# Two layers of a hybrid decoder on one core: the prompt's queries and keys are transposed in the projection, into the place of x, and the prompt's compression moves into retention

## The reference

```python
u = rmsnorm(x, norm_pre) @ w_in            # 3872 columns: ret q,k,v,g | nsa q,kv,gates | gdn qkv,...
# retention: 4 heads, a state carried over the tiles of the prompt, per sample for the samples
# gated DeltaNet: 4 heads, behind a convolution of width 4
# NSA, prompt: 8 query heads in 2 groups (4 heads share one key/value head), head size 64
k_c = compress(rows[:, :, 0]); v_c = compress(rows[:, :, 1])   # 31 blocks of 32 positions
o = gate0 * attend(q, k_c, v_c) + gate1 * attend(rope(q), k_sel, v_sel) + gate2 * attend(rope(q), k_win, v_win)
x = x + rmsnorm(concat(ret, nsa, gdn) @ w_out, norm_post)
```

## Time and profile before

| | |
|---|---|
| time, median of 3 runs | 2633.17 us (2610.85 to 2634.86) |
| profiled execution | 2642.13 us, its span 2640.5 us |
| mean granted TensorE clock of that execution | 0.854 |
| busy: PE / PEld / DVE / ACT / POOL | 84% / 63% / 50% / 28% / 11% |
| read from HBM, written | 223.17 MB, 24.97 MB |

### The profile page before, as it was taken

One profiled execution on the slowest core, in us unless ns is written; L12 is line 12 of the kernel. 1 busy time (PEld: TensorE's weight loads), 2 busy tenths in 40 slices (PEclk: granted clock), 3 DMA queues, 4 the chain that ended last, 5 costly groups with the idle time before them and its releaser, 6 DMA issues. The chain is left out here.

```text
span 2640.5 us, 35927 instructions
## 1 busy us (share of the span) xinstructions
PE 2229.7 (84%) x12280; PEld 1657.8 (63%) x12280; DVE 1321.1 (50%) x3088; ACT 730.7 (28%) x1512; POOL 302.4 (11%) x516
## 2 busy tenths in 40 slices
PE   6989748738999999997889896586499999999977
PEld 3644448737767888886354444486376678888863
DVE  1252566534654666654213434765355556666532
ACT  2120002103434454440212101111044445444302
POOL 0000000000013433420000000000000234334100
PEclk9999769756879999996989997687567889999859
DMA  4443010020027886851035330100300368868420
GB/s 148 147 151 113 26 35 1 1 79 7 1 52 168 192 188 152 181 124 72 2 113 168 137 109 10 35 1 2 84 1 1 89 150 191 179 152 190 107 72 36
DMA packets 175947, 242.04 MB, mean 92 GB/s; under 512 B 50118, under 2 KB 132838, under 8 KB 175084
## 3 DMA queue, kind: packets, MB, share of 16 engines
q1 hardware_dynamic: 151180, 172.51, 24.5%
q0 software_dynamic: 24576, 67.14, 10.8%
HBM read 223.17 MB, written 24.97 MB: 94 GB/s over the span
## 5 line engine op out<-in xcount | busy, mean ns | idle before, releaser
L601 PE MATMUL bank<-W,hT 128*128 128x512 f32 (+3 forms) x1152 | 449.0, 544 | 30.6 <-DMA W<-in_w_in 21.5
L1282 POOL DMA_DIRECT2D SHARED<-in_cache_nsa_kv x256 | 151.5, 592 | 2048.7 <-issue 734.4
L601 PEld LDWEIGHTS bank<-W,hT 128*128 128x128 f32 x1152 | 219.0, 195 | 230.8 <-issue 184.5
L1225 PE MATMUL bank<-XT,W 128*128 128x256 f32 (+1 forms) x768 | 250.8, 462 | 0.0
L1214 ACT ACTIVATE XT<-bank 128x512 f32<-128x512 f32 x256 | 140.3, 593 | 132.6 <-PE bank L1207 132.5
L1282 POOL DMA_DIRECT2D PS<-in_cache_nsa_kv x256 | 150.7, 589 | 140.6 <-issue 128.2
L1225 PEld LDWEIGHTS bank<-XT,W 128*128 128x128 f32 x768 | 134.9, 190 | 49.7 <-issue 36.9
L1207 PE MATMUL bank<-CF,RP 128*128 128x128 f32 x1024 | 146.9, 290 | 7.6 <-DVE RP L1195 6.9
L1708 PE MATMUL bank<-QBD,PS 128*128 128x64 f32 x1024 | 141.9, 287 | 0.0
L1501 DVE TENSOR_REDUCE mx<-bank 128x1 f32<-128x31 f32 (+4 forms) x192 | 74.6, 389 | 132.5 <-PE bank L1443 131.1
L1708 PEld LDWEIGHTS bank<-QBD,PS 128*128 128x128 f32 x1024 | 139.7, 210 | 0.7
(11 more groups left out here) (378 smaller groups left out, 3699.4 us busy)
## 6 DMA issues: line engine op xcount, KB each, us to landing
SHARED<-in_cache_nsa_kv SPq DMA_DIRECT2D x256, 128.0 KB, 6.1
SHARED<-in_cache_nsa_kv POOLq DMA_DIRECT2D x256, 128.0 KB, 5.3
PS<-in_cache_nsa_kv SPq DMA_DIRECT2D x256, 128.0 KB, 6.1
PS<-in_cache_nsa_kv POOLq DMA_DIRECT2D x256, 128.0 KB, 5.7
W<-in_w_in SPq DMA_DIRECT2D x48, 512.0 KB, 4.5
XS<-scratch_conv_p SPq DMA_DIRECT2D x24, 384.0 KB
PW<-in_state_nsa_win SPq DMA_DIRECT2D x16, 512.0 KB, 3.8
Wo<-in_w_out SPq DMA_DIRECT2D x4, 2048.0 KB, 11.8
```

The costliest lines, as they stand in the source:

```text
L601: return nc.tensor.matmul(bk((c * NTILE + t) % 8)[:, 0:b - a], hT[:, k, t * P:(t + 1) * P], W[:, k // 2, k % 2, 0:b - a], start=(k == 0), ...
L1225: mm = nc_(self.v).tensor.matmul(out, self.v['W1'][:, kv, s, :], seg[:, s], start=(s == 0), stop=(s == SEG // PAIRS - 1))
L1282: e.dma_start(where[side * HD:(side + 1) * HD, slot, :, :], A['cache_nsa_kv'][l, page].rearrange("(p r) a g d -> p r (a g d)", r=PAIRS)[:, ...
```

## The change

x leaves the core after its transposition: `X` is stored to `q_rot` and, for the sample rows, to `y_sample`, and `out_project` loads it back behind `w_out`. Its place holds `QT` [128, 2, 4, 512] and `KT` [128, 2, 512] until then. In `project`, the rotated queries of tiles 0 to 2 go to MIX, those of tile 3 to `QR`; bank 7 is taken from the ring (8 banks become 7) and 8 key transposes (beside chunk 7) and 32 query transposes (beside chunk 8) go through it, copied out by ScalarE. In `retention`, the prompt's compression and the loading of its weights run beside the tiles, at the places of the table `BESIDE`. The early stage of `prompt_attention` is gone. In its main stage both groups share one `KT` and one `KC`: group 0 in rows 0 to 63, group 1 in rows 64 to 127, so a score product has the 64 rows of its group. The branches run in the order 1, 2, 0.

```diff
@@ project
-    NC, RING = len(chunks), 4
+    NC, RING, BANKS, TURNS = len(chunks), 4, 7, 7
+    q_rows = lambda t: MIX[:, t, :].rearrange("p (i c) -> p i c", i=2) if t < 3 else QR[:, :, :]
@@ SP
+            e.dma_start(A['q_rot'].rearrange("(t p) d -> p t d", p=P), X[:, 0:4, :]).then_inc(kept, 16)
+            e.dma_start(O['y_sample'].rearrange("b t d -> (b t) d"), X[0:64, 4, :]).then_inc(kept, 16)
...
-                dve.wait(e, f"nqc{j}")
-                e.dma_start(A['q_rot'][j * P:(j + 1) * P, :], QR[:, :, :].rearrange("p i c -> p (i c)")).then_inc(rot, 16)
@@ ACT
+            copies(e, 6, 0)
+            e.wait_ge(kept, 32)
+            for t in range(4):
+                pe.wait(e, f"tk{t}")
+                act.done(e, f"tk{t}", nc.scalar.activation(KT[:, :, t * P:(t + 1) * P], bk(TURNS, 4)[:, 0:2, :], ACT.Copy))
+            copies(e, 7, 0)
+            for t in range(4):
+                for i in range(2):
+                    pe.wait(e, f"tq{t}{i}")
+                    act.done(e, f"tq{t}{i}", nc.scalar.activation(QT[:, i, :, t * P:(t + 1) * P], bk(TURNS, 4), ACT.Copy))
@@ PE
+            def key_turn(t):
+                dve.wait(e, f"kv2{t}")
+                if t:
+                    act.wait(e, f"tk{t-1}")
+                for i in range(2):
+                    mm = nc.tensor.transpose(bk(TURNS, 4)[:, i, :], U[t][:, NKV + 256 * (i + 1):NKV + 256 * (i + 1) + P], ident)
+            def query_turn(t, i):
+                dve.wait(e, f"nqc{t}")
+                act.wait(e, f"tq{t}0" if i else f"tq{t-1}1" if t else "tk3")
+                for r in range(R):
+                    mm = nc.tensor.transpose(bk(TURNS, 4)[:, r, :], q_rows(t)[:, i, r * P:(r + 1) * P], ident)
...
-                        if j == 0 and u >= 8:
-                            e.wait_ge(e_dve if u % 2 else e_act, (u - 8) // 2 + 1)
+                        if j == 0 and u >= BANKS:
+                            e.wait_ge(e_dve if (u - BANKS) % 2 else e_act, (u - BANKS) // 2 + 1)
...
+                        if c == 7 and j == 1 and t < 4:
+                            key_turn(t)
+                        if c == 8 and j < 2 and t < 4:
+                            query_turn(2 * j + t // 2, t % 2)
@@ retention
+    BESIDE = {("norm", 0): ["R0", "R1"], ("back", 1): ["T0", "T1", "X0", "X1"], ("back", 3): ["H0", "HT0"], ("norm", 3): ["A0", "HS0"],
+              ("back", 4): ["C0", "H1", "C0k", "HT1", "A1", "HS1"], ("norm", 4): ["C1", "C1k"]}
@@ retention, SP: after `gn` come the rows PG (2 DMAs), the wait for z3, W1 (8), W2 (4), B1 (1), then load_states as before
@@ retention, PE
+                    if x in ("H0", "H1"):
+                        if x == "H0":
+                            e.wait_ge(small, 13 * 16)
+                            dve.wait(e, "ss3m")
+                        else:
+                            dve.wait(e, "A0.p")
+                        cp.halves(e, pe, act, int(x[1]))
...
+                if t == 4:
+                    act.wait(e, "X1.p")
@@ retention, DVE, first
+            dve.link(e, "z3", nc.vector.memset(W2[:, :, :, :], 0.0))
+            dve.done(e, "z4", nc.vector.memset(HS[:, :, :], 0.0))
@@ delta: z3 and the 13 DMAs are gone
@@ prompt_attention: the early stage is gone; new_kv and first_pages go to the main stage
-    units = [(qt, br, h) for qt in range(4) for br in range(3) for h in range(NH)]
+    units = [(qt, br, h) for qt in range(4) for br in (FIRST, 2, LAST) for h in range(NH)]     # FIRST, LAST = 1, 0
...
-                kt = KCG[:, g, 0:n] if br == 0 else KT[:, g, br - 1, 0:n]
-                nc.tensor.matmul(sbank(u)[:, 0:n], QT[:, min(br, 1), r, qt * P:(qt + 1) * P], kt, start=True, stop=False)
+                o = g * HD
+                kt = KC[o:o + HD, 0:n] if br == 0 else KT[o:o + HD, br - 1, 0:n]
+                nc.tensor.matmul(sbank(u)[:, 0:n], QT[o:o + HD, min(br, 1), r, qt * P:(qt + 1) * P], kt, start=True, stop=False)
@@ out_project
+            e.dma_start(X[:, 0:4, :], A['q_rot'].rearrange("(t p) d -> p t d", p=P)).then_inc(back, 16)
+            e.dma_start(X[0:64, 4, :], O['y_sample'].rearrange("b t d -> (b t) d")).then_inc(back, 16)
...
             e.wait_ge(gain, 16)
+            e.wait_ge(back, 32)
```

More of the change, by code:

```diff
@@ L678, in retention @@
             dn += [f"ss{k}{j}" for k in range(4) for j in "ms"] if t == 4 else []
-    with stage(["dve_s", "act_s", "pe_s", "loaded", "gl", "outs"]) as (block, (dve_s, act_s, pe_s, loaded, gl, outs)):
+            an += [f"sq{t}"]
+        beside = BESIDE.get((what, i), [])
+        pn += [f"{x}.p" for x in beside if x in ("T0", "T1", "H0", "C0", "H1", "C1")]
+        an += [f"{x}.p" for x in beside if x in ("X0", "X1", "HT0", "HS0", "HT1", "HS1")]
+        dn += [{"C0k": "C0.p", "C1k": "C1.p"}.get(x, f"{x}.p") for x in beside if x in ("R0", "R1", "A0", "C0k", "A1", "C1k")]
+    with stage(["dve_s", "act_s", "pe_s", "loaded", "gl", "rows", "small", "outs"]) as \
+            (block, (dve_s, act_s, pe_s, loaded, gl, rows, small, outs)):
         dve = Steps(dve_s, dn)
-        act = Steps(act_s, [f"sq{t}" for t in TILES])
+        act = Steps(act_s, an)
         pe = Steps(pe_s, pn)
@@ L686, in _ @@
             e.dma_start(gn[:, :], A['ret_gn'][l].partition_broadcast(P)).then_inc(gl, 16)
+            for i in range(2):
+                e.dma_start(PG[:, i, :, :], O['kv_prompt'][l, 0].rearrange("(t p r) a g d -> t p r (a g d)", p=P, r=PAIRS)[i, :, :, 0:256]).then_inc(rows, 16)
+            dve.wait(e, "z3")
+            for kv in range(2):
+                for half in range(2):
+                    for r in range(PAIRS):
+                        e.dma_start(W1[r * HD:(r + 1) * HD, kv, :, half * HD:(half + 1) * HD],
+                                    A['cmp_w1'][l, kv].rearrange("(h s r) d e -> h r d s e", h=2, r=PAIRS)[half, r]).then_inc(small, 16)
+                for g in range(G):
+                    e.dma_start(W2[:, kv, g, g * HD:(g + 1) * HD], A['cmp_w2'][l, kv]).then_inc(small, 16)
+            e.dma_start(v['B1'][:, :], A['cmp_b1'][l].rearrange("k e -> e k"), allow_slow_non_contiguous=True).then_inc(small, 16)
             dve.wait(e, "z2")
@@ L710, in _ @@
                 QK, ATT, KDc = QK_[:, i % 2], ATT_[:, i % 2], KDc_[:, i % 2]
+                if what == "norm":
+                    beside(what, i)
                 if what == "front":
@@ L763, in _, with beside @@
             h3 = lambda ap: ap.rearrange("p (h c) -> p h c", c=HD)
+            def beside(what, i):
+                for x in BESIDE.get((what, i), []):
+                    if x in ("R0", "R1"):
+                        e.wait_ge(rows, 32)
+                        cp.side_by_side(e, dve, pe, int(x[1]), int(x[1]))
+                    if x in ("A0", "A1"):
+                        cp.join(e, dve, act, pe, int(x[1]))
+                    if x in ("C0k", "C1k"):
+                        cp.keep(e, dve, pe, int(x[1]))
             for what, i, t in ORDER:
```

219 lines of the change are left out of this document (81 added, 138 removed).

## The result

The changed kernel takes **2750.51 us** (median of four runs, 2749.22 to 2761.45), the kernel before 2633.75 (four runs, 2610.85 to 2634.86): ratio 1.046, 95% interval 1.041 to 1.051, 117 us slower. The forecast was 2715, range 2655 to 2742. The direction and the part of the clock came out as said, the size did not. The profiled execution took 2749.22 (span 2747.6), 107 us more than that of before; the table is made against these two.

What follows compares the result with a forecast made beforehand. TensorE and its clock bound the main stage. Per layer +68 + 6.2 + 5 − 0.7 = +78.5; both layers +157.0 − 78.2 = +78.8, giving 2721 or, by the median, 2712; said 2715, range 2655 to 2742.

Steps and rivals of the forecast that it cites:

- The main stage's clock: Main stage: the clock counts filled rows, so it stays at 1.2 GHz throughout; 234 against 166.1, +68 us per layer.
- the thin stretches: Earlier trace: clock fell during 64-row products at 83% busy, and stayed 0.50 through 13.7 us without idle, among 31-row products.
- The main stage's size: Main stage: durations stay, so units at 1.2 GHz give 225.9 us, plus some 8 for filling, draining, merges and barrier.
- the upper bound of 75: Main stage: upper end of its cost per layer, +75 us if merges expose more.
- The prediction's own sign: Main stage: the forecast is wrong if units at clock 0.50 last other than in the earlier trace.
- Retention: Retention: compression work beside the tiles costs +5 us per layer, between bounds of about 2 and nearly 10.
- the wait at A1: End of retention: VectorE waits at join A1 with the last norm queued behind it, some 3 us more.
- Projection: Projection: 40 transposes at 4.4 us and the lost bank at 1.8 us, +6.2 us per layer.
- the bank's wait: Projection, chunk 4: with seven banks TensorE's 5.51 us wait for a VectorE copy grows by 1.8 us.
- Early stage and output projection: Early stage goes whole, 78.2 us for both layers; x returns before its addition with 16 us of cover, costing nothing.
- Delta: Delta: loses its clearing of `W2`, −0.7 us per layer with the wait behind it.
- The second one: Main stage: the clock rises in 512-key units alone, giving back 70 us, 2645 by the median; chance 0.06.
- the case to which the first led: Main stage: the clock follows busy time alone, 0 in place of +136; 2585, or 2576 by the median; chance 0.10.

Runs made afterwards that it cites:

- experiments 1 and 2: The kernel before with 64-row score products and nothing else, 2802.97 us; then the changed kernel with 128-row score products put back, 2566.11 us.
- experiment 5: The changed kernel with the scores of two heads of one group issued together, then both masks: 2706.13 us, ratio 1.028.
- Experiments 8 and 9: Changed kernel, 128 rows for query tiles 0-1, cross-group pairs for 2-3; join A1 moved behind the last norm, 2549.51 us; then HT1 too, 2547.21 us.
- experiment 2: The changed kernel with 128-row score products put back, using keys padded with zeros: 2566.11 us, ratio 0.977.
- experiment 4: The kernel before with 64-row score products for the four heads of group 1 alone: 2676.31 us, ratio 1.017.

## Why the prediction was right in direction and short in size

**The main stage's clock** was right: 0.50 throughout, +68 or more per layer, and experiments 1 and 2 show it as cause, alone and reversed. Its evidence, the thin stretches, pointed the right way. That the clock counts rows alone is too simple: experiment 5, with the rows of the changed kernel and fewer changes, let it rise late. By the Trainium skill (TensorE: Matmul & The Clock Gate, "Part 1: The HAM clock gate") the clock depends on how busy TensorE has been; with 69.30 of 70 us busy at 0.50, and the profile's busy time taken for that, the trace does not agree.

**The main stage's size** is the step that failed: "Streamed columns, records and durations stay." They stay for a record, but not for what lies between two. Against the lengths of the earlier trace rows, two changes of rows per unit cost 0.25 to 0.31 us for 128 to 512 keys and 0.11 for a compressed one: 16 × (0.31 + 0.29 + 0.25 + 0.25) + 32 × 0.11 = 21 us per layer. With them 225.9 + 21 = 247, and 5 for filling and draining where I had put 8: 251.8. That is +86 for +68, 35 us over both layers, beyond the upper bound of 75 that I gave merges alone. The prediction's own sign, units at 0.50 that last other than in the earlier trace rows, came. The main stage before changes its rows only for the 31-row values of compressed units, and I did not look there for a price. It could be read there: from a 31-row value product to the score product 0.35 us (737.18 to 737.53), from a 128-row one 0.21 (741.74 to 741.96).

**Retention** was mis-sized by 1 to 2 us in this trace, where the same code took from 69.3 to 72.0 us in others: the transposes 1.4 for 1.7, the wait at A1 4.5 for 3. The first SiLU needs a function load of 1.28 us (366.58), ahead of the products that the join waits for; in the kernel before such a load stands at 593.26 in the early stage, and I did not count it. Experiments 8 and 9 place the cost: the tail is 8.8 us, and 7.2 with the queues in the better order.

**Projection** was right on the mean, and in part by luck in one trace: the new code took from 291.6 to 297.3 us over all traces, the old from 286.1 to 289.6, with means of 293.8 and 287.7, 6.1 apart (forecast 6.2). In layer 0 the bank's wait grew by 1.9 and the 40 transposes took 4.3 (forecast 4.4). Besides, the products of 512 columns took 2.3 us more (178.2 for 175.9) and the other waits 1.4 less. The longer wait left the clock down for longer, which I had not priced; the stretch around it, before and after:

```profile
136.00:152.00 16.00, 10.49 (x27) 4.22 (x26) 11.43 (x15) 1.93 (x3) 0.00 (x0) 0.89 0.38 125
```
```profile
136.00:152.00 16.00, 11.34 (x25) 4.83 (x26) 10.61 (x13) 1.93 (x3) 0.00 (x0) 0.68 0.39 125
```

In layer 1 the bank's wait grew by 2.1 (5.7 for 3.6), while the 256-column products took 14.9 us for 17.9: before, they had fallen into a stretch at the lower clock. **Early stage and output projection** were right.

**Delta** (+3.3, +0.9 for −0.7) **and the samples' attention** (−5.4, −4.9 for 0) were not forecast to move, and no code in the latter differs. That stage ranges from 450.4 to 463.5 us over the traces, with equal code and busy time of VectorE; its clock differs:

```profile
839.40:1290.40 451.00, 424.44 (x2918) 358.44 (x2918) 272.27 (x655) 195.78 (x312) 146.88 (x248) 0.95 0.69 155
```
```profile
806.20:1269.50 463.30, 439.36 (x2918) 372.60 (x2919) 272.56 (x655) 195.87 (x312) 146.73 (x248) 0.91 0.66 151
```

The first is the changed kernel, the second experiment 5. Where in the stage the clock falls differs from trace to trace; I have not found what sets it, and it stays open. The same may lie behind delta; that is argued, not shown. Its old code took from 205.8 to 209.8 us over the traces, the new from 206.2 to 210.7. The 10 us that the samples' attention gave were luck: without them the forecast would have missed by more.

**The rivals**: none came. (The second one's 2645 is 70 less than 2715; by the median, as its text says, it would be 2642.) But the case to which the first led, 2576 to 2585, is what experiment 2 gives (2566) when the rows are kept: the rest of the change, 15 us of new order among it, gains 64 us (2630.5 less 2566.1), and the 64-row products turn that into a loss of 117.

## What to carry to other kernels

Where TensorE is the bound, price a thinner product twice: by the granted clock, which fell from 0.77 to 0.50 with the same 864 records, and by its changes between row counts, 0.31 us for the two of a unit at 1.2 GHz. Zeros in the other rows took TensorE no time here and kept the clock; better still is work in both halves, two heads side by side. When a wait is moved behind other work, read all the queues that it passes: the join moved for nothing until ScalarE's half copy moved with it.

## What the runs showed of the hardware

- Two 64-row products in different halves of the array run at once: four records of 512 columns in 2.08 us at 1.2 GHz, 3.78 in one half. The Trainium skill says so (TensorE: Matmul & The Clock Gate, "Part 3: Packing small matmuls — row/col tiling"), and the trace agrees.
- The next product's weights are loaded under way behind a product of the same 128 rows (738.54 for a product at 739.39), and between two 64-row products of one half (in experiment 5 757.77 for a product at 758.62), but not from 64 rows to 128 or back (804.00 for 804.00; 801.99 for 802.00). The same section of the Trainium skill has the load overlap only where the row groups differ, though it also names a background weight buffer as a second case; these rows show the overlap where the row groups are the same.
- The clock, once up, stays up over units that did not raise it: 96 units of 64-row scores per layer left it at 0.50 in the changed kernel, and in experiment 4 four such units in a row ran at 2.4 GHz, 2.50 us each for 512 keys. Issued in pairs (experiment 5) 64-row units did raise it, at 772.8 us in layer 0, 188 us into the stage.
